# The gate of the state-space rounds formed by one VectorE instruction that reads PSUM, in place of two of GpSimd's and a copy of ScalarE's

## The reference

```
y = y + d_skip * xs
yg = y * silu(z)
yg = yg * rsqrt(mean(yg * yg over the group's 512 channels) + EPS)
ssd_branch = yg * norm_w
```

## Time and profile before

| | us |
|---|---|
| median of 3 runs | 1315.72 |
| lowest and highest | 1315.63, 1315.89 |
| the profiled execution | 1315.32 |
| its span, first to last instruction | 1313.6 |
| state-space rounds in it | about 181 to 255 |

### The profile page before, as it was taken

How to read it: one execution, slowest core, us unless ns; L and a number is a source line. 1 busy time by engine, 2 the same in 40 slices (tenths; PEclk the granted TensorE clock), 3 DMA queues, 4 the chain that set the end, 5 groups by cost and what they waited for, 6 DMA issues and landing times.

```text
span 1313.6 us, 18045 instructions
## 1 busy us (share of the span) xinstructions
PE 1278.9 (97%) x7149; PEld 644.1 (49%) x7149; DVE 472.1 (36%) x1110; ACT 340.1 (26%) x666; POOL 64.3 (5%) x73
## 2 busy tenths in 40 slices
PE   9999999999999999999999999999999999999997
PEld 7888888899983333333332333333332333333332
DVE  5978999987653111211112111111121111121112
ACT  4757777654441101011010011001010110111102
POOL 1000024322010000000000000000000000000000
PEclk9999999999999999999999999999999999999999
DMA  8333264556889999999999999999999999999996
GB/s 304 128 135 124 75 229 143 206 201 243 346 325 388 426 409 428 429 428 429 429 427 429 430 427 429 430 427 429 429 427 429 430 427 429 430 427 429 429 426 266
DMA packets 37939, 467.22 MB, mean 356 GB/s; under 512 B 4752, under 2 KB 4784, under 8 KB 9344
## 3 DMA queue, kind: packets, MB, share of 16 engines
q1 hardware_dynamic: 37600, 466.00, 85.6%
q10 hardware_dynamic: 288, 0.52, 0.1%
HBM read 465.43 MB, written 1.08 MB: 355 GB/s over the span
## 4 chain that ended last, share of the span: by engine, by line
PE 42%; DMA 27%; DVE 0%; issue 0%; SPq 0%; ACT 0%; DVEq 0%; ACTq 0%
PE bank L1528 39%; DMA ring<-wts_dram 27%; PE bank L1908 1%; PE bank L1902 1%; PE bank L1932 0%; SPq L424 0%; SPq L533 0%; DVE work L1522 0%; DVE work L1489 0%; ACT work L952 0%; DVE work L1433 0%; DVEq L106 0%; DVE work L1435 0%; ACT work L849 0%; PE bank L1892 0%
## 5 line engine op out<-in xcount | busy, mean ns | idle before, releaser
L1528 PE MATMUL bank<-ring,work 128*64 128x512 f32 (+2 forms) x2152 | 489.9, 587 | 21.9 <-DMA ring<-wts_dram 21.2
L1528 PE MATMUL bank<-work 128*64 128x512 f32 (+8 forms) x2216 | 433.5, 544 | 2.5 <-DVE work L1429 1.0
L1528 PEld LDWEIGHTS bank<-ring,work 128*64 128x64 f32 (+1 forms) x2152 | 156.7, 138 | 306.1 <-issue 262.3
L1528 PEld LDWEIGHTS bank<-work 128*64 128x64 f32 (+4 forms) x2216 | 147.5, 143 | 257.1 <-issue 245.7
L1456 DVE COPY work<-bank 128x256 f32<-128x256 f32 x30 | 12.7, 425 | 452.3 <-PE bank L1932 452.3
L1528 PE MATMUL bank<-hn_hi,split 128*128 128x256 f32 (+1 forms) x896 | 172.7, 288 | 1.4 <-DVE split L1039 1.4
L1528 PEld LDWEIGHTS bank<-hn_hi,split 128*128 128x128 f32 x896 | 141.3, 189 | 2.8 <-issue 2.3
L1528 PE MATMUL bank<-hn_lo,split 128*128 128x256 f32 (+1 forms) x448 | 127.2, 284 | 0.0
L1039 DVE TENSOR_TENSOR split<-ring,split 128x1024 fp32r<-128x1024 f32 x88 | 111.5, 1269 | 24.2 <-ACT split L640 23.9
L1433 DVE TENSOR_SCALAR work<-bank 128x512 f32<-128x512 f32 x32 | 22.1, 692 | 262.3 <-PE bank L1528 262.3
L880 ACT ACTIVATE work<-bank 128x512 f32<-128x512 f32 x31 | 18.5, 597 | 325.6 <-PE bank L1528 325.6
(11 more groups left out here) (307 smaller groups left out, 997.7 us busy)
## 6 DMA issues: line engine op xcount, KB each, us to landing
ring<-wts_dram SPq DMA_DIRECT2D x123, 2048.0 KB, 23.3
work<-wts_dram SPq DMA_DIRECT2D x63, 2048.0 KB, 25.3
ring<-slabs_dram SPq DMA_DIRECT2D x23, 2048.0 KB, 8.5
ring<-wts_dram SPq DMA_DIRECT2D x7, 1024.0 KB, 18.3
ring<-decay_rows SPq DMA_DIRECT2D x16, 256.0 KB, 3.4
work<-wts_dram SPq DMA_DIRECT2D x4, 1024.0 KB, 12.4
ring<-slabs_dram SPq DMA_DIRECT2D x2, 1152.0 KB, 6.3
work<-x_dram SPq DMA_DIRECT2D x3, 512.0 KB, 12.3
```

The lines of the kernel that those rows point to most:

```text
L1528: return pe.matmul(o, lhsT, rhs, start=start, stop=stop)
```

## The change

In each of the 16 rounds, L594 and L597 on GpSimd and the copy L808 on ScalarE are gone, and so is the tile `zcopy`'s use. ScalarE's tanh now counts up a semaphore of its own, `z_tanh`. VectorE has a new instruction between L1272 and L1276, which reads z(c) from its PSUM bank and forms `(ztanh + 1) * z` into `zw`. It is this instruction that counts up `proj_read` for z(c). ScalarE's first gate unit waits for the last of these counts.

```diff
@@ gpsimd
-            for c in range(NX):
-                pool.wait_ge(proj_read, U["z", c] + 1)
-                link(pool.tensor_scalar(ztanh[:, c % 2, :], ztanh[:, c % 2, :], 1.0, None, ALU.add))
-                if c:
-                    pool.wait_ge(y2_ready, c)
-                pool.tensor_tensor(zw, ztanh[:, c % 2, :], zcopy[:, c % 2, :], ALU.mult).then_inc(zw_ready, 1)
@@ scalar, z_of(c)
-                a.activation(ztanh[:, c % 2, :], ps[:, 0:SEQ], ACT.Tanh, scale=0.5)
-                a.activation(zcopy[:, c % 2, :], ps[:, 0:SEQ], ACT.Copy).then_inc(proj_read, 1)
+                a.activation(ztanh[:, c % 2, :], ps[:, 0:SEQ], ACT.Tanh, scale=0.5).then_inc(z_tanh, 1)
@@ scalar, gate units
                 if u < 16:
+                    if u == 0:
+                        a.wait_ge(proj_read, U["z", NX - 1] + 1)
                     ps = unit("g", u)
@@ vector, round c
                 d.scalar_tensor_tensor(yv, xT[:, c, NMETA:L], v("d_skip", c, 1), bank[3 + 2 * (c % 2)][:, 0:SEQ], ALU.mult,
                                        ALU.add).then_inc(ssdy_read, 1)
+                d.wait_ge(z_tanh, c + 1)
+                d.scalar_tensor_tensor(zw, ztanh[:, c % 2, :], 1.0, bank[U["z", c] % 2][:, 0:SEQ], ALU.add,
+                                       ALU.mult).then_inc(proj_read, 1)
                 d.wait_ge(ssdy_read, c + 1)
-                d.wait_ge(zw_ready, c + 1)
+                d.wait_ge(proj_read, U["z", c] + 1)
                 d.tensor_tensor(y2T[:, c, :], yv, zw, ALU.mult).then_inc(y2_ready, 1)
```

More of the change, by code:

```diff
@@ L300, in meta_ssd_mla_moe @@
         cb_done = sem("cb_done")
-        zw_ready = sem("zw_ready")
+        z_tanh = sem("z_tanh")
         diff2_ready = sem("diff2_ready")
```

## The result

| | median us | against before |
|---|---|---|
| before | 1315.68 (4 runs, 1314.86 to 1315.89) | |
| the change | 1325.71 (4 runs, 1325.37 to 1325.91) | 1.0075, interval 1.0063 to 1.0087 |

The change makes the kernel 10.0 us slower. The forecast was 1326.3. The profiled execution took 1325.64 us, with a span of 1323.8 us, 10.2 more than before, and 1.8 us outside it.

The account below looks back on a forecast made before the run. In the rounds TensorE and VectorE were both nearly full; the change makes a loop through both. 3.26 + 6.52 + 0.79 = 10.57 us on the profiled 1315.32 gives 1325.9, median 1326.3 us, range 1323.8 to 1329.8.

Parts of the forecast that it names:

- Which wait: State-space rounds: z(c + 2) waits for the new VectorE instruction, which stands behind L1272's wait for round c's y product.
- The loop's length: Each round, z unit through y product, L1272 and new instruction to next z unit: 2.96 + 1.16 + 0.40 + 0.47 + 0.15 = 5.14 us.
- VectorE's own work hidden, GpSimd's relief worth nothing: Rounds: VectorE needs 3.31 or 3.65 of 4.27 us, waiting some 0.6; relief of about 0.7 us a round gains nothing.
- The first round: Unit z(2) starts at 188.54 and round 1's y product at 191.50 instead of 188.24: 3.26 us later.
- The brackets: Sign in the new trace: TensorE's z units from round 1 on carry idle brackets of some 0.3 and 0.8 us in turn.
- The clock: Rival: the first round's 3.3 us idle gap lowers TensorE to 1.2 GHz, 2.96 us more, 1329.3 us; chance 10%.
- The exit: First gate unit behind the rounds starts 2.18 us after the last y product instead of 1.39: 0.79 us more.
- Handed on to the end: Behind the rounds, the delay of 10.57 us passes through the gate and expert stages to the end, 1 for 1.
- VectorE's relief as the deciding thing: Rival: VectorE sets the rounds' pace, so less GpSimd contention gains at most 2.0 us, 1313.7 us; chance 4%.
- the experts' stream absorbs the delay: Rival: the delay arises, but the experts' weight stream, with DMA share 0.99, takes it up: 1316 us; chance 4%.
- a longer loop than the computed one: Rival: VectorE is not back in time, 5.35 us a round instead of 5.14, 3 us more, 1329.3 us; chance 4%.

Follow-up runs that it names:

- experiment 1: Kernel before, plus a TensorE wait for the previous round's y2 ahead of each z unit of rounds 1 to 15 and the first gate unit: 1327.82 us, ratio 1.0093.
- experiment 2: Changed kernel with ScalarE's copy of z kept to free the bank, and VectorE's gate formed from that copy: 1314.00 us, ratio 0.9991.
- experiment 3: Changed kernel with its new VectorE instruction moved up, ahead of the wait for the y product: 1313.78 us, ratio 0.9986.
- experiment 6: Changed kernel with one useless VectorE instruction (0.34 us) added behind y2 in every round: 1326.36 us, ratio 1.0078.
- experiment 4: Changed kernel with 12 useless 128-column matmuls on TensorE in the gap ahead of unit z(2): 1323.88 us, ratio 1.0064.
- 8: Kernel of experiment 3 with the gate of round 0 alone moved ahead of the diff step: 1314.43 us, ratio 0.9991.

## Why the prediction was right, step by step

- **Which wait.** Right, and the runs show it from both sides: the wait alone costs 12 us (experiment 1), and the new work without the late release costs nothing (experiment 2), nor do the very instructions of the change when the gate stands ahead of the wait (experiment 3).
- **The loop's length.** 5.14 forecast, 5.06 measured. The one step that was off is the new instruction itself: 0.41 us, not 0.47. I took the length of L1272 because it also reads PSUM. That was the wrong likeness: by the rows in the last section the longer time goes with L1272's scalar, which is read from SBUF, and not with PSUM. The lower bound, L1276, was the better neighbour. From VectorE's end to TensorE it is 0.06 us rather than 0.15, and from the unit's start to the product 3.03 rather than 2.96; the two together are what they were. Fourteen rounds make that 1.06 us less than forecast, 5.46 instead of 6.52.
- **VectorE's own work hidden, GpSimd's relief worth nothing.** Right: L1233 takes 0.98 or 0.99 us in every round, where the earlier trace rows have 1.52, and VectorE spends the gain waiting, at brackets of some 0.42 us in rounds with a sum of squares or a variance step and 0.76 in plain ones. The prediction's own sums give 4.27 - 3.65 = 0.62 and 4.27 - 3.31 = 0.96; its "0.6" is the smaller, and both came out 0.2 too large. Experiment 6 shows that 0.34 us more are hidden.
- **A row misread.** The round of the earlier trace rows is called one nearly without GpSimd. It is not; GpSimd's pair ran in it, and the second of them took 2.31 us where 0.74 is its median:

```profile
202.19 0.95 POOL L594 TENSOR_SCALAR work<-work 128x256 f32<-128x256 f32 x1 [3.67 <-ACT work L808]
203.22 2.31 POOL L597 TENSOR_TENSOR work<-work 128x256 f32<-128x256 f32 x1
```

So in that round it was GpSimd that was stretched and not VectorE. The figure taken from it, 3.81 us for VectorE's round undisturbed, held: with GpSimd silent and the gate's 0.34 us added it is the 4.15 of experiment 3.
- **The first round.** From the y product of round 0 to the unit z(2), 187.51 - 182.79 = 4.72 us; forecast 188.54 - 183.66 = 4.88, so right but for the instruction's length and a little.
- **The brackets.** Of the signs named beforehand, idle brackets of 0.3 and 0.8 us in turn did not come: they are 0.44 and none. The loss per round is there all the same, 0.23 and 0.70 us by the starts; the prediction did not allow for the 0.25 us by which the brackets come out shorter.
- **The clock.** Wrong in its weight. I gave it 10%, since nothing in the trace of before showed a fall, and left it out of the sum. It happened, for 2.3 us (3.0 had been the price), and experiment 4 shows the gap as the cause. The trace of before could not refute it: its longest gap in this stage was 0.71 us, and the change makes one of 3.1. A row with a gap of 0.7 says nothing about one four times as long.
- **The exit.** 0.79 forecast, 0.64 measured.
- **Handed on to the end.** Right to 0.4 us out of 10.6.
- **Why the total fits better than its parts.** The parts in the trace sum to 11.56 us against 10.57 forecast, with the clock's 2.29 missing from the forecast and 1.3 too much in the other steps. The profiled execution began the rounds 0.87 us early, which the change does not explain: over the traces of this study round 0's product starts between 182.79 and 183.99 us, in kernels whose code up to there is alike. So that the forecast for the median is only 0.6 us off is partly luck.

Of the rivals, VectorE's relief as the deciding thing is refuted for this order of instructions. With an early release it may show, as the 0.14% of experiment 3 and the 0.09% of experiments 2 and 8, the latter two with intervals that reach 1. That the experts' stream absorbs the delay is refuted by the chain, and a longer loop than the computed one by the 5.06 us.

## What to carry to other kernels

When a read that frees a buffer is moved to another engine, look at what that engine waits for just ahead of it, not at what the read costs: here 0.41 us of work put behind one wait cost 10 us, and the same work four instructions further up in the same engine's order cost nothing (1.6 us less than before, just outside the noise). Write the new loop down as a sum (product, reader, release, next producer) and compare it with the producer's own round; here it could be worked out from rows of the old trace to within 2%. And where a change makes a gap on TensorE longer than any that the old trace has, keep the clock in the sum.

## What the runs showed of the hardware

- The granted clock fell to 0.50 in all the traces with a first gap of 2.73, 3.12, 3.13 and 3.58 us, and the unit behind took 5.3 to 5.4 us instead of 3.0. In the same kernels gaps of 0.29 to 1.04 us later in the stage left it at 1.00, and in experiment 4, where matmuls without use filled all but 0.45 us, it stayed at 1.00. The Trainium skill (TensorE: Matmul & The Clock Gate, Part 1: The HAM clock gate) has an idle TensorE drop to 1.2 GHz and come back once it is busy; these traces agree: in the changed kernel the granted clock is 0.50 up to 192 us, 0.84 from 192 to 194 and 1.00 from there on, with TensorE at work again from 187.51. What a gap between 1.04 and 2.73 us does was not tried.
- A VectorE `scalar_tensor_tensor` on 128x256 float32 took 411 to 415 ns with a constant as scalar and one operand in PSUM (L1270, 16 times), and 414 to 421 with a constant and both in SBUF (the gate of experiment 2). With a scalar read from SBUF for each partition it took 476 to 482 ns, with one operand in PSUM (L1267) as with both in SBUF (L1307 in the norm stage of the changed kernel). So the 65 ns go with the scalar, and reading PSUM made no difference. The operations (add, multiply) are not the same in all four, so that they have a part in it is not excluded.
- GpSimd's two instructions stretched VectorE's work by 0.35 to 0.74 us in each round of the kernel before from 204.84 us on, up to 251.38, by the starts of L1272 and without the 0.31 us that VectorE once waited for L597. Without them the round with one instruction more is 4.15 us instead of 4.50. Where GpSimd was the one stretched, as above, VectorE lost nothing.
